# One transformer layer in float32 pairs: the way into the MLP, its first tile, and the last stores

## The reference

```python
mix = jnp.concatenate([na_o, da_o], axis=-1) @ w_out[layer]
x = x + g1[:, None] * mix
h2 = rms_norm(x, norm2_g[layer]) * (1 + sc2[:, None]) + sh2[:, None]
ff = (jax.nn.silu(h2 @ w_gate[layer]) * (h2 @ w_up[layer])) @ w_down[layer]
x = x + g2[:, None] * ff
return rms_norm(x, final_g)
```

## Time and profile before

| | us |
|---|---|
| runs, median of 3 (lowest, highest) | 2189.14 (2188.84, 2189.52) |
| the profiled execution, its own time | 2188.42 |
| its span | 2186.8 |
| TensorE busy in it | 2157.0 |
| VectorE busy | 1736.8 |
| ScalarE busy | 893.7 |
| GpSimd busy | 254.2 |

### The profile page before, as it was taken

How to read it: one execution, slowest core, us unless ns; L and a number is a source line. 1 busy time by engine, 2 the same in 40 slices (tenths; PEclk the granted TensorE clock), 3 DMA queues, 4 the chain that set the end, 5 groups by cost and what they waited for, 6 DMA issues and landing times.

```text
span 2186.8 us, 33010 instructions
## 1 busy us (share of the span) xinstructions
PE 2157.0 (99%) x11054; PEld 1823.8 (83%) x11054; DVE 1736.8 (79%) x2441; ACT 893.7 (41%) x1253; POOL 254.2 (12%) x307
## 2 busy tenths in 40 slices
PE   8999999999999998999999999999999999999997
PEld 6888888877777886888888888888888888888887
DVE  7897776788877888788888888888888754999434
ACT  4434333455562114344444444444444433434222
POOL 6012222100022330000000000000000100000222
PEclk9999999999999999999999999999999999999999
DMA  9995666544427882233333333333333743434333
GB/s 351 354 369 162 208 221 217 185 160 170 145 96 290 294 280 91 97 121 115 120 119 129 120 115 121 119 129 120 115 120 120 254 150 125 135 101 165 114 97 111
DMA packets 140614, 362.25 MB, mean 166 GB/s; under 512 B 22072, under 2 KB 54984, under 8 KB 140048
## 3 DMA queue, kind: packets, MB, share of 16 engines
q1 hardware_dynamic: 129184, 322.22, 43.8%
q0 software_dynamic: 10224, 38.61, 4.9%
q10 hardware_dynamic: 1152, 0.73, 0.1%
HBM read 341.80 MB, written 19.71 MB: 165 GB/s over the span
## 4 chain that ended last, share of the span: by engine, by line
PE 96%; DVE 2%; DMA 1%; issue 1%; ACT 0%; SPq 0%; POOL 0%; DVEq 0%; ACTq 0%; POOLq 0%
PE PS L1088 18%; PE P L1088 12%; PE S L1088 6%; PE T L1088 6%; PE P L787 4%; PE PS L787 4%; PE PS L789 4%; PE PS L788 4%; PE P L789 4%; PE P L788 4%; PE T L787 2%; PE T L788 2%; PE T L789 2%; PE T L1134 2%; PE T L1136 2%; PE T L1135 2%
## 5 line engine op out<-in xcount | busy, mean ns | idle before, releaser
L1778 DVE TENSOR_TENSOR W_lo<-raw,W_hi 128x1024 fp32r<-128x1024 f32 (+1 forms) x189 | 229.5, 1214 | 167.2 <-ACT W_hi L1238 165.5
L1238 ACT ACTIVATE W_hi<-raw 128x1024 fp32r<-128x1024 f32 (+1 forms) x189 | 193.5, 1024 | 392.5 <-PE T L789 113.6
L2296 DVE TENSOR_TENSOR W_lo<-raw,W_hi 128x1024 fp32r<-128x1024 f32 x191 | 233.4, 1222 | 54.6 <-ACT W_hi L1562 50.6
L1562 ACT ACTIVATE W_hi<-raw 128x1024 fp32r<-128x1024 f32 x191 | 202.0, 1060 | 178.8 <-PE P L1088 94.5
L2299 DVE TENSOR_TENSOR raw<-raw 128x1024 f32<-128x1024 f32 x192 | 233.8, 1219 | 0.1
L1562 ACT ACTIVATE H<-raw 128x1024 fp32r<-128x1024 f32 x145 | 152.9, 1055 | 167.7 <-DVE raw L2299 93.6
L1088 PE MATMUL P<-H,W_hi 128*128 128x512 f32 x760 | 190.3, 392 | 0.1
L2296 DVE TENSOR_TENSOR H<-raw,H 128x1024 fp32r<-128x1024 f32 x145 | 176.5, 1218 | 0.0
L787 PE MATMUL P<-H,W_hi 128*128 128x512 f32 x416 | 170.1, 409 | 5.8 <-DVE H L2031 2.6
L787 PE MATMUL PS<-H,W_hi 128*128 128x512 f32 x432 | 174.0, 403 | 0.9 <-DVE W_lo L1778 0.8
L789 PE MATMUL PS<-H,W_lo 128*128 128x512 f32 x432 | 169.2, 392 | 0.0
(11 more groups left out here) (411 smaller groups left out, 4515.1 us busy)
## 6 DMA issues: line engine op xcount, KB each, us to landing
raw<-in_w_gu SPq DMA_DIRECT2D x176, 512.0 KB, 3.3
raw<-in_w_in SPq DMA_DIRECT2D x72, 512.0 KB, 4.2
adar<-in_w_ada SPq DMA_DIRECT2D x72, 512.0 KB, 4.2
att<-in_w_ada SPq DMA_DIRECT2D x32, 1024.0 KB, 10.9
att<-in_w_ada SPq DMA_DIRECT2D x56, 512.0 KB, 4.7
raw<-in_w_out SPq DMA_DIRECT2D x32, 512.0 KB, 5.1
raw<-in_w_down SPq DMA_DIRECT2D x32, 512.0 KB, 3.5
raw<-in_w_down SPq DMA_DIRECT2D x32, 448.0 KB, 3.3
```

The lines of the kernel that those rows point to most:

```text
L1238: act.activation(w_parts(slot)[0][:, 0:cols], raw[:, raw_slot * PW:raw_slot * PW + cols], ACT.Copy).then_inc(hi_done, 1)
L1562: act.activation(form_parts(slots[a])[0], raw_form(FORM_RAW[a]), ACT.Copy).then_inc(hi_done, 1)
L1778: dve.tensor_tensor(lo[:, 0:cols], raw[:, raw_slot * PW:raw_slot * PW + cols], hi[:, 0:cols].bitcast(F32), ALU.subtract).then_inc(lo_done, 1)
L2296: dve.tensor_tensor(lo, raw_form(FORM_RAW[a]), hi.bitcast(F32), ALU.subtract).then_inc(lo_done, 1)
```

## The change

1. **First gate and up tile.** With h2 = X * s2 * rstd + shift, its product with a weight is (W x (X * s2)) * rstd + W x shift, since rstd is one factor per token, that is per column of the result. For the first NB = 5 row tiles TensorE takes X * s2, which needs no norm. Their high parts are made by ScalarE (five ACTIVATE with scale s2) and their low parts by VectorE (`x_low`), to the same places of H. The results go to the banks Sb, the other eleven row tiles (true h2, order 5 to 15) to Tb[1] and Mb. The sum for the norm (`token_sum`) now stands between the second and the third of the five; the ten filling products are gone.
2. **The shift** of the five row tiles is a product of its own: twenty matmuls of 2 columns (high and low part of the shift, `shift_parts`) to `shift_bank`.
3. **The exit.** VectorE multiplies both Sb banks by rstd, adds up the two columns of each shift bank (`shift_sum`), adds the bank of the other row tiles; Silu takes the gate's shift as its bias, the last pass the up's.
4. **h2 of row tiles 0 to 4** is made last (H2_ORDER), after the first tile is on its way; the first pair of f = 1 takes row tiles 8 to 15 first, then 5, 6, 7 and 0 to 4, and SyncE loads its two halves the other way round.
5. **A fourth weight place** W3, over the rows 3 and 4 of w_ada in `att`, for the second half of up. The first tile's four pieces have a place each.
6. **Modulation.** Shift2 and scale2 are finished ahead of the last `out_pair`; two of the last eight w_ada rows and gate2 are taken after the first tile. In the last `out_pair` the split of piece 31 goes ahead of rows 3 to 5.
7. **The units of T** are placed by the table MAKES: one in f = 1, five in f = 2, two in f = 3.
8. **The last stores** of the second half are five instead of four: row tiles (14, 15), (0, 1), (2 to 4), (5 to 8), (9 to 13). The first, third and fifth are issued by ScalarE's queue.
9. The loops over f on TensorE and SyncE are written out.

```diff
+NB = 5
+H2_ORDER = tuple(range(NB, KT)) + tuple(range(NB))
+MAKES = {(1, 3): (0,), (2, 1): (1, 2), (2, 2): (3,), (2, 3): (4, 5), (3, 1): (6,), (3, 2): (7,)}
...
+        W3 = nc.alloc_sbuf_tensor_at("W3", [P, 2 * PW], F32R, offset=overlay + 6 * S * 4)
...
-        BATCHES = (((0, 7), (7, DONE), (DONE, KT)), ((DONE, KT), (0, 5), (5, 10), (10, DONE)))
+        BATCHES = (((0, 7), (7, DONE), (DONE, KT)), ((DONE, KT), (0, 2), (2, 5), (5, 9), (9, DONE)))
...
-            token_sum(1)
-
-            pe.wait_ge(lo_done, MLP0 + 1)
-            for i in range(10):
-                pe.matmul(Pb[1][:, :], W_hi[:, 0:P], W_hi[:, 0:S], start=True, stop=True)
-            pair(MLP0, Pb, lambda k: pe.wait_ge(mlp_ready, k + 1))
-            with pe.Fori(1, NPL) as f:
+
+            for k in range(NB):
+                if k == 2:
+                    token_sum(1)
+                for b in range(2):
+                    if k == 0:
+                        pe.wait_ge(lo_done, MLP0 + b + 1)
+                    if b == 0:
+                        pe.wait_ge(mlp_ready, k + 1)
+                    tile(Sb[b], w_parts(2 * b), k, H_hi, H_lo, k, k == 0, k == NB - 1)
+            pe.wait_ge(mod_ready, 7)
+            for k in range(NB):
+                pair_k = shift_parts[:, 2 * k:2 * k + 2]
+                for b in range(2):
+                    wh, wl = [w[:, k * P:k * P + P] for w in w_parts(2 * b)]
+                    pe.matmul(shift_bank[b], wh, pair_k, start=k == 0, stop=False)
+                    pe.matmul(shift_bank[b], wl, pair_k, start=False, stop=k == NB - 1)
+            for k in range(NB, KT):
+                for b in range(2):
+                    n = 2 * (k // HALF) + b
+                    if k in (NB, HALF):
+                        pe.wait_ge(lo_done, MLP0 + n + 1)
+                    if b == 0:
+                        pe.wait_ge(mlp_ready, k + 1)
+                    mm = tile(rest_bank[b], w_parts((0, 2, 1, 3)[n]), k % HALF, H_hi, H_lo, k, k == NB, k == KT - 1)
+                    if k % HALF == HALF - 1:
+                        mm.then_inc(used, 1)
+            for f in range(1, NPL):
...
 ScalarE
             for f in range(1, NPL):
-                for j in range(1, 4):
+                for j in range(3 if f == 1 else 1, 4):
                     split_gu(f, j)
-                    if 3 * f - 4 + j < HALF:
-                        t_high_half(3 * f - 4 + j)
+                    for u in MAKES.get((f, j), ()):
+                        t_high_half(u)
...
 VectorE, last out_pair
                 if final:
+                    split(n + 3, 1, 3)
                     ada_out(3)
                     ada_out(4)
-                    split(n + 3, 1, 3)
                     ada_out(5)
-                    ada_out(6)
-                    ada_out(7)
                     split(n + 4, 0, 0)
+                    split(MLP0 + 1, 2, 1)
+                    x_low(0)
+                    x_low(1)
...
+            for i in range(KT - NB):
+                h2_low(i)
+                if i == 1:
+                    split(MLP0 + 2, 1, 2)
+                elif i == 2:
+                    split(MLP0 + 3, 3, 3)
+                elif i == 9:
+                    split_gu(1, 0)
+            dve.wait_ge(used, MLP0 + 2)
+            for b in range(2):
+                dve.tensor_tensor(E1[b], Sb[b][:, :], rstd[:, :], ALU.mult).then_inc(mod_ready, 1)
+            for b in range(2):
+                dve.tensor_reduce(shift_sum[:, b:b + 1], shift_bank[b], AX.X, ALU.add).then_inc(mod_ready, 1)
+            dve.wait_ge(used, MLP0 + 3)
+            dve.wait_ge(mod_ready, 11)
+            dve.tensor_tensor(E1[0], E1[0], rest_bank[0][:, :], ALU.add).then_inc(mod_ready, 1)
+            split_gu(1, 1)
+            for i in range(KT - NB, KT):
+                h2_low(i)
+                if i == KT - 3:
+                    split_gu(1, 2)
+            dve.wait_ge(used, MLP0 + 4)
+            dve.tensor_tensor(E1[1], E1[1], rest_bank[1][:, :], ALU.add).then_inc(mod_ready, 1)
+            dve.wait_ge(mod_ready, 13)
+            dve.wait_ge(gated, 1)
+            dve.scalar_tensor_tensor(ftile, E1[1], shift_sum[:, 1:2], gate, ALU.add, ALU.mult).then_inc(f_made, 1)
...
             for f in range(1, NPL):
-                for j in range(1, 4):
+                for j in range(3 if f == 1 else 1, 4):
                     split_gu(f, j)
-                    u = 3 * f - 4 + j
-                    if u < HALF:
+                    for u in MAKES.get((f, j), ()):
                         make_t(u)
-                    if 0 < u <= HALF:
-                        t_low(u - 1)
+                        if u:
+                            t_low(u - 1)
```

More of the change, by code:

```diff
@@ L671, in _ @@
                 load(j, w_gu[PAIR_SRC[j]], PW)
-            with sp.Fori(1, NPL) as f:
+            for f in range(1, NPL):
                 for j in range(4):
                     sp.wait_ge(lo_done, 4 * f + (MLP0 + j - 3))
-                    load(j, w_gu[bass.ds(4 * f + j, 1)].rearrange("a p n -> (a p) n"), PW)
+                    load(j, w_gu[4 * f + (j if f > 1 else (1, 0, 2, 3)[j])], PW)
             def load_form(f, slot):
@@ L1062, in _ @@
+            for f in range(1, NPL):
                 for g in range(2):
-                    pe.wait_ge(f_made if g else gated, f)
+                    if f > 1:
+                        pe.wait_ge(f_made if g else gated, f)
                     for h in range(2):
-                        piece(4 * f + (MLP0 + 2 * g + h), h, Pb[g], H_hi, H_lo, half_kts(h), KT - 1)
+                        n = 4 * f + (MLP0 + 2 * g + h)
+                        if f + g > 1:
+                            piece(n, h, Pb[g], H_hi, H_lo, half_kts(h), KT - 1)
+                            continue
+                        ks = list(half_kts(1)) if h == 0 else list(range(NB, HALF)) + list(range(NB))
+                        pe.wait_ge(lo_done, n + 1)
+                        for k in ks:
+                            if k < NB:
+                                pe.wait_ge(mlp_ready, NB + KT - NB + k + 1)
+                            mm = tile(Pb[g], w_parts(h), k % HALF, H_hi, H_lo, k, k == HALF, k == NB - 1)
+                        mm.then_inc(used, 1)
@@ L1769, in _ @@
                 act.activation(half_cols(rstd, h), half_cols(root, h), ACT.Exp, scale=-0.5).then_inc(root_made, 1)
+            n_made = len(BATCHES[0]) + 1
+            for n, (k0, k1) in enumerate(BATCHES[1]):
+                n_made += 2 if k0 == DONE else 1
+                if n % 2 == 0:
+                    act.wait_ge(y_made, n_made)
+                    act.dma_start(out_half_of(k0, k1, 1), token_half(k0, 1, k1 - k0)).then_inc(y_out, 16)
         @block.vector
@@ L2250, in h2_low @@
-            def h2_low(k):
-                dve.wait_ge(h2_hi, k + 1)
-                dve.scalar_tensor_tensor(H_lo[:, k * S:k * S + S], E0[k % 4], mod[:, 3 * KT + k:3 * KT + k + 1],
+            dve.wait_ge(kept, heads_kept + KT // 2 - 2)
+            add_mod(3 * KT, 5 * KT, 2)
+            dve.scalar_tensor_tensor(s2[:, :], mod[:, 4 * KT:5 * KT], 1.0, gn2[:, :], ALU.add, ALU.mult).then_inc(mod_ready, 1)
+            sp_hi, sp_lo = [shift_parts[:, :].rearrange("p (k w) -> p k w", w=2)[:, :, w] for w in range(2)]
@@ L2253, in h2_low @@
+            def h2_low(i):
+                scaled(i + 2)
+                k = H2_ORDER[i]
+                dve.wait_ge(h2_hi, NB + i + 1)
+                dve.scalar_tensor_tensor(H_lo[:, k * S:k * S + S], E0[i % 4], mod[:, 3 * KT + k:3 * KT + k + 1],
                                          H_hi[:, k * S:k * S + S].bitcast(F32), ALU.add, ALU.subtract)\
                     .then_inc(mlp_ready, 1)
-            scaled(0)
-            scaled(1)
-            for k in range(KT):
-                if k + 2 < KT:
-                    scaled(k + 2)
-                h2_low(k)
-                if k == HALF + 1:
-                    split(MLP0 + 3, 2, 3)
@@ new lines, in _ @@
+            for i in range(KT - NB, KT):
+                h2_low(i)
+                if i == KT - 3:
+                    split_gu(1, 2)
+            dve.wait_ge(used, MLP0 + 4)
+            dve.tensor_tensor(E1[1], E1[1], rest_bank[1][:, :], ALU.add).then_inc(mod_ready, 1)
+            dve.wait_ge(mod_ready, 13)
+            dve.wait_ge(gated, 1)
+            dve.scalar_tensor_tensor(ftile, E1[1], shift_sum[:, 1:2], gate, ALU.add, ALU.mult).then_inc(f_made, 1)
+            for v in range(6, AO):
+                dve.wait_ge(first_in[v], 16 * (KT // 2 - 1))
+                dot(first[v], v, first_dot)
```

101 lines of the change are left out of this document (70 added, 31 removed).

## The result

The changed kernel takes 2196.04 us (median of 8 runs, 2193.58 to 2197.0), the kernel before 2188.74 in the 8 runs beside them (2188.02 to 2189.52): a ratio of 1.0032 with an interval of 1.0021 to 1.0043, that is slower by 7.3 us. The forecast was 2188.4 with a range to 2191.6. The profiled execution took 2197.0 us, its span is 2195.4 (before: 2188.42 and 2186.8).

What follows compares the result with a forecast made beforehand. TensorE, busy 99%, was taken as the bound, with VectorE nearly as loaded. Passage -1.8, clock +1.6 and tail -0.55 us sum to -0.75 on the median 2189.14: 2188.4 us, range 2185.0 to 2191.6.

Steps and rivals of the forecast that it cites:

- Piece 31: Last piece of the output projection: its low part is made earlier, so TensorE's hole ahead of it goes, -0.9 us.
- The norm's chain: After the projection: row tile 15 updated at 831.2 against 831.96, first multiplication by the norm column 836.2 against 836.85.
- the sign: Stated failure test: the forecast fails as a whole if row tile 15's update comes later than 831.96.
- The first tile's remaining row tiles: First gate and up tile: VectorE's work on eleven row tiles lets the next tile start at 857.1, -6.8 us.
- The twenty shift products: Narrow products in the first tile: 2.4 us, costing nothing inside 3.9 us that TensorE would otherwise wait for VectorE.
- rival 3: Narrow shift products cost 0.46 us each and decide: +5.3 us, all kept, 2193.7 us; chance 0.08.
- Units bunched: Five T units in f = 2: TensorE waits 0.9 us ahead of piece 10, 4.2 ahead of piece 12; gain there -1.8.
- Rival 2: No wait in f = 2, VectorE finishes its units earlier; the -6.9 us gain stays whole, 2181.7 us; chance 0.12.
- The clock: After the 4.2 us wait in f = 2 TensorE's products run at half clock for a while, +1.6 us.
- rival 1: The clock stays up in the long wait in f = 2, giving 2186.8 us; chance 0.20.
- The tail: Last stores of the second half: smaller first batches fill a hole between stores, -0.55 us.
- Rival 4: At the exit the larger last store makes the tail give nothing or cost 0.4 us: 2189.0 to 2189.4; no separate chance.

Runs made afterwards that it cites:

- x6: x2 with the small shift2 and scale2 operations moved behind the first split of the last out_pair; 2189.43 us, ratio 0.9998.
- x7: Changed kernel with 128 bytes more padding, the small modulation operations moved and one T unit per split; 2183.05 us, ratio 0.9968.
- x10: x7 with the twenty narrow shift products issued twice; 2186.12 us, ratio 0.9985.
- x8: Changed kernel with sixteen unused products of ones with ones while TensorE waits ahead of pair f = 3; 2193.88 us, ratio 1.0017.
- x1: Kernel before with 128 unused bytes ahead of the overlay (att and what is laid over it), nothing else; 2195.98 us, ratio 1.0035.
- x4: Kernel before with only the change's last stores (five batches, three from ScalarE's queue); 2188.36 us, ratio 0.9997.
- x5: Kernel before with 128 unused bytes ahead of H, so everything moves together; 2188.89 us, ratio 0.9995.
- x9: Kernel before with 128 unused bytes between X and W_hi, moving weight places, raw and overlay while H and X stay; 2210.63 us, ratio 1.0099.
- x2: Changed kernel with 128 bytes more, so the overlay has its old place modulo 256; 2190.36 us, ratio 1.0008.
- x3: Changed kernel with the eight T units placed one behind each split; 2188.51 us, ratio 1.0001.
- x11: x7 with four narrow products behind each of the five row tiles instead of one block of twenty; 2183.44 us, ratio 0.9973.

## Why the prediction was wrong

It forecast -0.75 us and a range to 2191.6; +7.3 was measured. The steps in their order:

- *Piece 31*, -0.9: right. Between 820 and the update of row tile 15 the delay falls from 3.58 to 2.77.
- *The norm's chain*: the order and the lengths held. The update came at 834.73 and not at 831.2, and the prediction said that it fails as a whole if this comes later than 831.96. The 3.5 us are the start of the run (1.1), growth in attention (1.0), 0.4 in the projection and piece 29's wait (1.0). So the sign fired, but an absolute time of one trace is a poor sign: 1.1 of it is the start of that run.
- *The first tile's remaining row tiles*: 25.9 us from the update to piece 4 worked out, 25.8 measured.
- *The twenty shift products*: 0.12 us each taken, 0.11 measured, 2.15 in all; rival 3 (0.46 each) fell. That they lie in a cover was right for this kernel; that they may pull down the clock (x6, x7, x10) was not thought of.
- *Joining at the exit*: no wait of the second tile's pieces is in the trace. Right.
- *Units bunched*: 0.9 and 4.2 worked out, 1.00 and 3.98 shown as idle. Rival 2 fell. From the update to piece 12 it is 74.8 us, worked out 74.6 (the terms as written add up to 0.2 less).
- *The clock*: the kind was right, rival 1 fell; the term of 1.6 was mis-sized, x8 and the steps give 2.2 to 2.4 for the changed kernel. I had taken the length of the slow stretch from the earlier trace rows, seven steps; here it was ten and a part at either end, and in x6, behind the same wait, six (1.5 us). What the prediction reads from the earlier trace rows, that gaps of 2.30 and 2.10 us are still short enough for a full clock, was luck of one trace: x1, x4, x5 and x9 fell to half clock there.
- *The tail*: -0.55 worked out, -0.58 measured, and x4 agrees. Rival 4 fell.
- *Modulation*, part 6, got no price at all. It was 1.0 us: three operations of 5 to 16 columns, counted as nothing because they are tiny, ahead of a split that TensorE waits for, beside GpSimd. That VectorE was slow at two places was in the earlier trace rows; what it ran beside there, GpSimd's square and sum from 820.97 to 825.05, is not in the prediction.
- **The step that failed** was not written down: that instructions outside the passage and the tail take the same time as before. The diff adds two arrays of 26 columns in all, and I read them as a matter of the shift products. They moved the area of T1 to T3 by 128 bytes: products with T start 233.6 ns apart in place of 226.7, and the loops with operands in that area take 5.9 us more by the traces; x1 puts 7.1 us on it by medians, x2 takes 5.7 back. With the place repaired (x2) the time is 2190.36, inside the range.

The sum with what was measured: -0.75, +1.0 for the modulation, +0.8 for the clock, +1.1 for the start of the profiled run, +0.4 for the wait at 690 and +5.9 for the placement (1.0 in attention, 4.9 from the sets on) is 8.5 us, against 8.6 in the span. The modulation and the placement were put at nothing without a reason. In the medians the start of one run weighs less: 7.3.

What stays open: why the distance matters, and on which bits of it. 128 bytes were tried at three places and 256 at one (x2); other distances, and the group of T4 in x9, were not followed up. When the clock falls stays open too: the same instructions kept it in one run and lost it in another. Whether x7 gains 1.6 us when both the narrow products' clock and the cover behind them are dealt with wasn't tried either.

## What to carry to other kernels

A new small array is a change to every operand allocated behind it. Compare the list of allocations of both kernels, and where a large operand has moved, try it with padding before the change itself is judged; here 128 bytes cost 5.7 to 7.1 us, about as much as the whole change gains when all is repaired (5.5 to 7.1). On an engine that feeds the one that bounds the time, price small operations by the neighbour they run beside, not by their columns, and place work that may wait behind the next thing that is waited for, one unit at a time.

## What the runs showed that was not expected

- A product of 512 columns lasts 392 or 395 ns, or 389 and 395, by where its operand lies against its weights (128 bytes to or fro); the start-to-start time goes from 226.7 to 233.6 ns. Moving everything together (x5) costs nothing, moving the weights away from H (x9) 21.4 us.
- An operation of VectorE on 5 columns took 1.24 us and one on 16 columns 0.90, ending with GpSimd's operation; the same operation on 5 columns took 0.17 when GpSimd had just ended (x6), and a cast of 5 columns 0.16.
- A block of twenty products of two columns, 2.15 us with no gap in it, was followed by half clock for 3.3 us in x6 and x7, but not in the changed kernel, x2, x3 and x8; forty of them went to half clock inside the block (0.21 us apart in place of 0.11). Four at a time between wide products (x11) left the clock up in the one run profiled.
- Behind the same wait of 2.30 us the clock stayed full in the profiled run of the kernel before and was at half in x1, x4, x5 and x9.
- Sixteen products of 128 columns, queued where TensorE would have waited 4 us, kept the clock up and were worth 2.2 to 2.4 us.
